# Attention heads and the first feed-forward pair cycle in another order, and a head's output processed in halves

## The chip, the cores and the metric

The kernel runs on one core of one Trainium2 chip. The metric is the device time of one execution in microseconds (us). A core has a matrix engine (TensorE, PE in the profile), three elementwise engines (VectorE = DVE, ScalarE = ACT, GpSimd = POOL) and queues for transfers; SyncE (SP) only issues transfers. The engines run at the same time, and wait for each other by semaphores.

## The reference

Two layers of an encoder over 576 tokens (512 of a prompt and 64 of a sample that also reads 128 cached keys), width 1024, in float32. Each layer is an attention part and a SwiGLU part:

```python
# layer 0: 8 latent-attention heads (mla) and 8 differential heads (diff) side by side
x = x + concat(mla(norm(x)), diff(norm(x))) @ w_out
x = x + (silu(norm(x) @ w_gate) * (norm(x) @ w_up)) @ w_down
# layer 1: 8 heads that attend to the keys an indexer selected (dsa)
x = x + dsa(norm(x)) @ w_out
x = x + (silu(norm(x) @ w_gate) * (norm(x) @ w_up)) @ w_down
# inside a diff head, after its two softmax maps were combined into one (p0 + (-lam) p1):
b_out = rmsnorm(b_out, g_subln, 1e-5) * (1 - lam_init)
```

## The kernel before

The program is written out by hand for each engine: five streams of instructions in program order, joined by semaphores. All of an engine's order is the order in which the code calls its functions. Nothing is reordered.

**Precision.** A float32 matrix product is made of three passes. Every operand is split into a high part (`WH`, `Qh`, `Kh`, `Vh`, `MIXh`, `HH`, made by ACT with a copy) and a low part (`WL`, `Ql`, `Kl`, `Vl`, `MIXl`, subtracted by POOL or DVE), and PE adds high x high, low x high and high x low in an accumulator. 576 tokens are two halves of 288 (`HALF`), so a pass over one weight tile is a pair of matmuls, shown as 128x288 x2.

**Heads.** Heads 0 to 7 are mla, 8 to 15 diff, 16 to 23 dsa. `attention(h)` runs in 8 slots. In slot s it makes the scores of token tile s (`head_scores`, result `S`), turns the probabilities `PR` of an earlier tile by transposes (`T<-IDN,PR`, line 1457 for the last tile), and projects a piece of the next head's q, k or v from its weights (`prepare`, line 1206; tables `CHUNKS`). In other slots come the output projection tiles of an earlier pair of heads (`output_tile`, added to `X` on DVE), the transposes of the next head's keys (`keys_to_tokens`: its new keys `YK` and the cached keys `KC`), and for diff heads the sum and root of the sub-norm (`subnorm_sum`, `subnorm_rows`). A projection leaves PSUM by DVE (`write_projection` to `YQ`, `YK`, `YV`), is split by ACT and POOL (`job`), and only then can scores use it. `acc.group(..., use=...)` picks the PSUM accumulator of a projection (ACC0, ACC1), which must be read out before its next use. DVE also takes row maxima (line 2659), the two maps' combination (`mix_maps`, line 2677) and low parts (`PTl`, line 2684). POOL issues the loads of the cached keys of the next head from its own queue (`load_cached_keys`, line 3242).

**End of an attention part (tail).** The last head's output is copied to `BO`, normed in head 15 (line 2709), split into `MIXh` and `MIXl` over all 576 tokens, and multiplied as the second half of the output projection (`second_half`, line 1527).

**Feed-forward part.** It makes the gate (`G`) and up (`U`) products of 22 blocks of the hidden size. The first two blocks are plain products (`PLAIN`), the others are made in pairs by seven products of half-sized sums (Strassen's form): sums of weights (`mix`, named S1 to S4, in `T` and `S`), split into WH and WL (`seven_high` on ACT, `seven_low` on DVE, line 2860), and sums of tokens (`token_sum` into `XD`, split into `TB`, lines 2892 to 2909). ACT copies a finished product to `TC` (`seven_copy`, line 2161). The first pair's cycle must make all four token sums. POOL multiplies silu(gate) `SG` by `U` into `HF` and splits it into `HH`.

Of the kernel before, what the change touches and what calls it, by code (L numbers as in the profile page):

```python
# [202 lines left out]

def build(nc, a, outs, scratch):
# [54 lines left out]

    VALUES_SHORT = (2, 8, 10, 18, 19, 21, 23)  # L260

    def plan_attention(h):
# [5 lines left out]
        for s in range(SLOTS):  # L268
            finished = []
            c = chunks(g)[s] if g is not None else None  # L270
# [25 lines left out]
            if s == 3 and h % 16 and kind_of(h - 1) == "diff":  # L296
                group("bs", h - 1, use=SHORT)
# [9 lines left out]
            if c:  # L307
                what, k0, k1, total = c
                if k0 == 0 and what not in ("v", "ps") or (k0 == 0 and what == "v" and kind_of(g) != "mla"):
                    if kind_of(g) != "mla":  # L310
                        unit(what, g, end=(what, g), in_slot=True)
                    elif what == "q":
                        unit("q", g, cols=QLT * P, end=("q", g), in_slot=True)
                    elif what == "k":
                        unit("kv", g, cols=2 * KLT * P, end=("v", g), in_slot=True)
                    else:
                        unit("pe", g, cols=2 * QLT * P, end=("ps", g), in_slot=True)
                if k1 == total:
                    group(what, g, use=SHORT if (what == "v" and g in VALUES_SHORT) or (what == "q" and g == 18) else LONG)
                    if kind_of(g) != "mla":  # L320
                        finished.append((what, g))
                    elif what in ("q", "v", "ps"):
                        finished.append(({"v": "kv", "ps": "pe"}.get(what, what), g))
            if h < 16 and g is not None and s == k_job_slot(g) == 5:
                jobs.add("k", g)
            if out_tile(h, s):
# [5 lines left out]
                group("wo", pair_out, m, use=OUT_PAIRS[h][m] if h in OUT_PAIRS else SHORT)  # L332
            begins.append((("slot", h, s), len(units.names) - 1, set(used_up)))
# [22 lines left out]
    def plan_pairs(layer, part):  # L356
# [17 lines left out]
        for c in range(c0, n + 1):  # L374
# [34 lines left out]
            if this:  # L409
# [4 lines left out]
                add(mixes, "S4", c)  # L414
                add(sums, "c11", c)
# [4 lines left out]
            if this:  # L420
                if c + 1 < n:
# [157 lines left out]
    with ctx:  # L579
# [170 lines left out]
        Y_MADE = {"q": 1, "k": 2, "v": 3}  # L750
        setup_c, setup_d = sem("setup_c"), sem("setup_d")
# [314 lines left out]
        def job_of(name):  # L1066
# [17 lines left out]
            if w == "o":  # L1084
                return BO[:, g % 2, :], MIXh[:, g % 2, :], MIXl[:, g % 2, :]

# [103 lines left out]
        def _(pe):  # L1190
# [324 lines left out]
            def second_half(p, m, low):  # L1515
# [4 lines left out]
                if low:  # L1520
# [3 lines left out]
                for left in (wh,) if low else (wh, wl):  # L1524
                    for b in range(2):
# [1928 lines left out]
```

## Time and profile before

| | before |
|---|---|
| time, median of 3 runs | 1730.51 us (1728.37 to 1733.53) |
| the profiled execution: time | 1732.16 us |
| its span in the profile | 1730.3 us |
| PE busy | 1678.6 us, 97% |
| DVE, ACT, POOL busy | 64%, 46%, 34% |
| mean granted PE clock | 0.992 of full speed |

The span is what the profiler saw of the execution; 1.9 us of the time lie outside it. The granted clock is the TensorE clock in parts of full speed. In the timelines a row ends with the idle time ahead of it and the instruction that ended it. A wait for several semaphores is put down to the one that came last by the profile, and that name can be wrong.

### The profile page before, as it was taken

To read this page: it belongs to the slowest core of one execution; us is meant where nothing else is said; L and a number is where in the kernel's file an instruction comes from. 1 tells how busy PE (TensorE), PEld (TensorE's weight loads), DVE (VectorE), ACT (ScalarE), POOL (GpSimd) and SP (SyncE) were. 2 spreads that over 40 slices of the span, in tenths; PEclk is the share of its full clock that TensorE was granted. 3 is DMA by queue.
4 is the path that set the end of the run, shared out by engine and by line. 5 is a ranking of instruction groups with operands and counts; after the bars stand their busy time and mean duration, and the time that the engine had idled before them with its cause. 6 is when DMAs were issued, how large, how long until landed. Compare 5 with 4: busy or idle time off the path is not lost.

```text
span 1730.3 us, 31752 instructions
## 1 busy us (share of the span) xinstructions
PE 1678.6 (97%) x12337; PEld 1617.3 (93%) x12345; DVE 1114.3 (64%) x2086; ACT 803.5 (46%) x1522; POOL 584.6 (34%) x442
## 2 busy tenths in 40 slices
PE   7999999999999999999999999999999999999998
PEld 6889999889898899999999999899989999999998
DVE  4656655555556698478467679633457974884776
ACT  4355555354545555245335445543456551552453
POOL 3344344355443122012102248474451230121122
PEclk9999999999999999999999999999999999999999
DMA  7221132332233123223323242332322332333231
GB/s 195 61 54 56 52 98 68 85 83 73 73 87 91 49 62 110 86 73 98 110 62 100 55 115 69 97 95 78 94 85 67 86 110 62 98 107 89 74 90 64
DMA packets 252104, 145.45 MB, mean 84 GB/s; under 512 B 21934, under 2 KB 242156, under 8 KB 251956
## 3 DMA queue, kind: packets, MB, share of 16 engines
q1 hardware_dynamic: 247080, 135.41, 27.6%
q0 software_dynamic: 4032, 7.77, 1.7%
q8 instruction: 100, 1.64, 0.4%
q14 instruction: 48, 0.39, 0.1%
q10 hardware_dynamic: 844, 0.24, 0.1%
HBM read 130.69 MB, written 15.32 MB: 84 GB/s over the span
## 4 chain that ended last, share of the span: by engine, by line
PE 82%; DVE 10%; ACT 3%; issue 3%; POOL 1%; DMA 1%; SPq 0%; DVEq 0%; ACTq 0%
PE ACC L1206 39%; PE ACC L1586 7%; PE ACC L1588 7%; PE ACC L1587 7%; PE T L1206 3%; PE ACC L1467 2%; PE S L1442 2%; PE S L1206 2%; DVE SCO L2732 2%; DVE TOP L2729 1%; ACT PR L2016 1%; PE S L1588 1%; PE S L1586 1%; PE S L1587 1%; PE S L1418 1%
## 5 line engine op out<-in xcount | busy, mean ns | idle before, releaser
L1206 PE MATMUL ACC<-XGh,WH 128*128 128x288 f32 x1024 | 233.6, 310 | 7.5 <-DVE YK L2585 2.1
L3170 POOL TENSOR_TENSOR WL<-RAW,WH 128x1024 fp32r<-128x1024 f32 (+3 forms) x84 | 180.4, 2150 | 156.9 <-ACT WH L1892 156.7
L3320 POOL TENSOR_TENSOR HF<-SG,U 128x576 f32<-128x576 f32 x44 | 66.6, 1515 | 477.7 <-ACT SG L2189 412.1
L1206 PE MATMUL ACC<-XGh,WL 128*128 128x288 f32 x1024 | 221.0, 298 | 0.0
L1206 PE MATMUL ACC<-XGl,WH 128*128 128x288 f32 x1024 | 220.6, 297 | 0.0
L1586 PE MATMUL ACC<-TB,WH 128*128 128x288 f32 x640 | 189.9, 297 | 5.1 <-DVE WL L2860 4.5
L1892 ACT ACTIVATE WH<-RAW 128x1024 fp32r<-128x1024 f32 (+3 forms) x159 | 153.1, 971 | 81.7 <-PE ACC L1206 43.7
L1588 PE MATMUL ACC<-TB,WL 128*128 128x288 f32 x640 | 189.4, 296 | 0.0
L1587 PE MATMUL ACC<-TB,WH 128*128 128x288 f32 x640 | 189.1, 296 | 0.0
L1206 PE MATMUL ACC<-HH,WH 128*128 128x288 f32 x1032 | 179.3, 295 | 0.0
L1206 PEld LDWEIGHTS ACC<-XGh,WH 128*128 128x128 f32 x1024 | 163.7, 191 | 14.2 <-DVE YK L2585 2.6
L1206 PEld LDWEIGHTS ACC<-XGh,WL 128*128 128x128 f32 x1024 | 165.9, 190 | 0.0
L1206 PEld LDWEIGHTS ACC<-XGl,WH 128*128 128x128 f32 x1024 | 165.8, 190 | 0.0
L1206 PEld LDWEIGHTS ACC<-HH,WH 128*128 128x128 f32 x1032 | 151.3, 188 | 0.0
L2016 ACT ACTIVATE PR<-SX,STAT 128x128 f32<-128x128 f32 (+4 forms) x160 | 85.7, 536 | 131.2 <-DVE STAT L2659 127.6
L1586 PEld LDWEIGHTS ACC<-TB,WH 128*128 128x128 f32 x640 | 120.8, 189 | 6.6 <-DVE WL L2860 4.9
L2423 DVE TENSOR_TENSOR X<-ACC,X 128x576 f32<-128x576 f32 x89 | 66.7, 752 | 89.1 <-PE ACC L1206 85.2
L2407 DVE TENSOR_TENSOR WL<-RAW,WH 128x1024 fp32r<-128x1024 f32 (+2 forms) x75 | 96.3, 1285 | 41.9 <-ACT WH L1892 41.6
L1588 PEld LDWEIGHTS ACC<-TB,WL 128*128 128x128 f32 x640 | 121.1, 189 | 0.0
L1587 PEld LDWEIGHTS ACC<-TB,WH 128*128 128x128 f32 x640 | 121.0, 189 | 0.0
L3322 POOL TENSOR_TENSOR HH<-HF,HH 128x576 fp32r<-128x576 f32 x44 | 67.8, 1541 | 137.6 <-ACT HH L2198 137.6
L1206 PE MATMUL ACC<-HH,WL 128*128 128x288 f32 x516 | 110.1, 294 | 0.0
(459 smaller groups left out, 4342.3 us busy)
## 6 DMA issues: line engine op xcount, KB each, us to landing
RAW<-in_w_gate_dram SPq DMA_DIRECT2D x44, 512.0 KB, 3.9
RAW<-in_w_up_dram SPq DMA_DIRECT2D x44, 512.0 KB, 4.6
RAW<-in_w_down_dram SPq DMA_DIRECT2D x32, 512.0 KB, 4.1
RAW<-in_w_in_even_dram SPq DMA_DIRECT2D x29, 512.0 KB, 5.1
RAW<-in_w_in_odd_dram SPq DMA_DIRECT2D x28, 512.0 KB, 4.4
RAW<-in_w_out_even_dram SPq DMA_DIRECT2D x16, 512.0 KB, 4.2
RAW<-in_w_down_dram SPq DMA_DIRECT2D x16, 384.0 KB, 3.5
RAW<-in_w_out_odd_dram SPq DMA_DIRECT2D x8, 512.0 KB, 5.0
```

Of the source, the lines that this page charges most:

```text
L1206: ins = pe.matmul(out[0:m, 512 * b:512 * b + width], left, right[:, b * width:(b + 1) * width], start=(first and part == 0), stop=(last an ...
L1442: ins = pe.matmul(out[0:r, 0:w], left, right, start=(i == 0), stop=(i == len(products) - 1))
L1586: pe.matmul(out, hi[:, w], xh, start=first and k == 0, stop=False, skip_group_check=not first)
L1587: pe.matmul(out, hi[:, w], xl, start=False, stop=False, skip_group_check=not first)
L1588: ins = pe.matmul(out, lo[:, w], xh, start=False, stop=k == 3, skip_group_check=not first)
L1892: act.activation(WH[slot][:, 0:n], RAW[slot][:, 0:n], ACT.Copy).then_inc(w_hi, 1)
L2016: act.activation(PR[m][0:r, n % 2, 0:w], SX[m][0:r, 0:w], ACT.Exp, bias=STAT[0:r, n % 2, m:m + 1], scale=-1.0, accum_out=STAT[0:r, n % 2, ...
L2407: dve.tensor_tensor(WL[slot][:, 0:n], RAW[slot][:, 0:n], WH[slot][:, 0:n].bitcast(F32), ALU.subtract).then_inc(w_lo, 1)
L2423: return lambda out: dve.tensor_tensor(two(X[:, m, :]), halves(out), two(X[:, m, :]), ALU.add)
L3170: pool.tensor_tensor(WL[slot][:, 0:n], RAW[slot][:, 0:n], WH[slot][:, 0:n].bitcast(F32), ALU.subtract).then_inc(w_lo_pool, 1)
L3320: pool.tensor_tensor(HF[:, q, :], SG[:, q, :], U[:, q, :], ALU.mult).then_inc(h_out, 1)
L3322: pool.tensor_tensor(HH[:, m, 1, :], HF[:, q, :], HH[:, m, 0, :].bitcast(F32), ALU.subtract).then_inc(h_lo, 1)
```

## The change

Nine places change; the arithmetic and the number of matmul passes do not.

1. Head 0: the q projection of head 1 goes ahead of the scores of slot 0 (`share_first`), and the q projection of head 2 moves from head 1's slot 0 to head 0's slot 5 (`share`). Accumulators of k of head 1 and q of heads 2 and 18 are chosen by `SHORT_TOO`.
2. Diff heads: POOL issues the load of the next head's cached keys behind the split of Vl instead of ahead of it.
3. Diff heads 8 to 14 write `YK` in slot 5 ahead of the turned probabilities' low part (`keys_early`).
4. Head 15: the sub-norm sum of head 14 moves behind the output tile of slot 3; its slot 5's addition to X goes ahead of `PTl`.
5. Head 16: the chunk v (4:6) of head 18 goes ahead of the scores of slot 3, and `YK` is written a slot later.
6. Head 22: the addition to X of slot 5 goes ahead of `PTl`.
7. Both tails: the last head's output is normed, split and multiplied in two halves of the tokens.
8. First pair cycle: the copies of the two plain `U` blocks go from DVE to ACT; token sum 3 and the next WG split go ahead of other DVE work; ACT copies the second product to `TC` ahead of S4's split.
9. POOL's first HF waits until the four token sums are split (`tb_lo`).

```diff
+def share(h, s):
+    if (h, s) == (0, 5):
+        return 2, "q", 0, QLT, QLT
+    g = prepared_in(h)
+    if g is None or (h, s) == (1, 0):
+        return None
+    c = chunks(g)[s]
+    return c and (g, *c)
+def share_first(h, s):
+    return (h, s) in ((0, 0), (16, 3))
...
             def attention(h):                              # PE
                 for s in range(SLOTS):
+                    c = share(h, s)
+                    if share_first(h, s):
+                        prepare(*c[:4])
                     if s < TOK_TILES:
                         head_scores(h, s)
...
-                    if g is not None and chunks(g)[s]:
-                        what, k0, k1, _ = chunks(g)[s]
-                        prepare(g, what, k0, k1)
+                    if c and not share_first(h, s):
+                        prepare(*c[:4])
...
+                    if (h, s) == (15, 3):
+                        subnorm_sum(14)
...
                 for low in (False, True):                  # PE, tail
-                    for m in range(halved):
-                        second_half(h - 1, m, low)
+                    for b in range(2):
+                        for m in range(halved):
+                            second_half(h - 1, m, low, b)
...
+            def take_plain_up(layer, m):                   # ACT
+                act.wait_ge(acc_done, acc.made("u", layer, m))
+                act.wait_ge(acc_free, acc.made("g", layer, m))
+                act.activation(two(U[:, m, :]), halves(pair(acc.at("u", layer, m))), ACT.Copy).then_inc(acc_free, 1)
...
-                return s == 5 and (h in (2, 4, 6) or h == 23)
+                return s == 5 and h in (2, 4, 6, 15, 22, 23)
+
+            def keys_early(h, s):                          # DVE
+                return s == 5 and kind_of(h) == "diff" and prepared_in(h) is not None
...
+            def last_norm(h):                              # DVE, tail
+                dve.wait_ge(acc_done, acc.made("bb", h))
+                rows = pair(acc.at("bb", h))
+                for b, (signal) in enumerate((tail_out, acc_free)):
+                    c = slice(b * HALF, (b + 1) * HALF)
+                    dve.scalar_tensor_tensor(out=BO[:, h % 2, c], in0=BO[:, h % 2, c], scalar=GSUB[:, 0:1],
+                                             in1=rows[:, c], op0=ALU.mult, op1=ALU.mult).then_inc(signal, 1)
...
-                    if s == 4 and x is not None and kind_of(h) != "mla" and h != 16:   # POOL
+                    if s == 4 and h > 16 and x is not None:
                         load_cached_keys(x)
...
                     if s == 4 and early_output(h) is not None:
                         job("o", early_output(h))
+                    if s == 4 and x is not None and kind_of(h) == "diff":
+                        load_cached_keys(x)
...
+                        if m == 0 and not part:
+                            pool.wait_ge(tb_lo, 4 * layer + 4)
```

On PE, at the start of head 0 (`QGh` is the latent of q, `WH_55` the weights of head 1's q), the order before is:

```order
L1345 MATMUL T<-IDN_67,BO_85 128x64
L1442 MATMUL S<-Kh_98,Qh0_94 128x128
L1442 MATMUL S<-Kl_99,Qh0_94 128x128
L1442 MATMUL S<-Kh_98,Ql0_96 128x128
L1442 MATMUL S<-KPEh_105,QPE_114 128x128
L1442 MATMUL S<-KPLE_106,QPE_114 128x128
L1344 MATMUL T<-IDN_67,YL_132 128x128 x2
L1345 MATMUL T<-IDN_67,BO_85 128x64
L1344 MATMUL T<-IDN_67,YL_132 64x128 x2
L1345 MATMUL T<-IDN_67,BO_85 64x64
L1206 MATMUL ACC0<-QGh_110,WH0_55 128x288 x2
L1206 MATMUL ACC0<-QGl_111,WH0_55 128x288 x2
```

and of the changed kernel, from the last of the three times that the projection's three passes are issued:

```order
L1235 MATMUL ACC0<-QGh_110,WH0_55 128x288 x2
L1235 MATMUL ACC0<-QGl_111,WH0_55 128x288 x2
L1235 MATMUL ACC0<-QGh_110,WL0_58 128x288 x2
L1471 MATMUL S<-Kh_98,Qh0_94 128x128
L1471 MATMUL S<-Kl_99,Qh0_94 128x128
L1471 MATMUL S<-Kh_98,Ql0_96 128x128
L1471 MATMUL S<-KPEh_105,QPE_114 128x128
L1471 MATMUL S<-KPLE_106,QPE_114 128x128
L1373 MATMUL T<-IDN_67,YL_132 128x128 x2
```

The nine rows of the projection, which began behind the transposes of `YL`, now stand ahead of the five rows of scores. The line numbers of the second fence are those of the changed file, here and below.

On POOL, in head 8, slots 4 and 5, the order before is:

```order
L3177 TENSOR_TENSOR Ql1_97<-YQ_91,Qh1_95 128x576
L3170 TENSOR_TENSOR WL0_58<-RAW0_52,WH0_55 128x1024
L3242 DMA KC_104<-in_cache_diff_k_dram 128x128
L3177 TENSOR_TENSOR Vl_101<-VF_102,Vh_100 128x768
L3170 TENSOR_TENSOR WL1_59<-RAW1_53,WH1_56 128x1024
```

and of the changed kernel:

```order
L3268 TENSOR_TENSOR Ql1_97<-YQ_91,Qh1_95 128x576
L3261 TENSOR_TENSOR WL0_58<-RAW0_52,WH0_55 128x1024
L3268 TENSOR_TENSOR Vl_101<-VF_102,Vh_100 128x768
L3333 DMA KC_104<-in_cache_diff_k_dram 128x128
L3261 TENSOR_TENSOR WL1_59<-RAW1_53,WH1_56 128x1024
```

The load of `KC` and the split of `Vl` change places; behind them stands a `WL` split in both.

On ACT, in the first pair cycle of layer 0, from the split of S12 on, the order before is:

```order
L2181 ACTIVATE WH1_56<-T 128x1024
L2203 ACTIVATE TB_148<-XD_146 128x1152
L2161 ACTIVATE TC_144<-ACC0 128x288
L2181 ACTIVATE WH2_57<-S 128x512
L2181 ACTIVATE WH3_62<-RAW1_53 128x512
L2181 ACTIVATE WH0_55<-RAW2_54 128x1024
L2181 ACTIVATE WH2_57<-S 128x512
L2161 ACTIVATE TC_144<-ACC0 128x288
```

and of the changed kernel:

```order
L2228 ACTIVATE WH1_56<-T 128x1024
L2301 ACTIVATE U_142<-ACC1 128x576
L2250 ACTIVATE TB_148<-XD_146 128x1152
L2208 ACTIVATE TC_144<-ACC0 128x288
L2228 ACTIVATE WH2_57<-S 128x512
L2228 ACTIVATE WH3_62<-RAW1_53 128x512
L2228 ACTIVATE WH0_55<-RAW2_54 128x1024
L2208 ACTIVATE TC_144<-ACC0 128x288
L2250 ACTIVATE TB_148<-XD_146 128x1152
L2228 ACTIVATE WH2_57<-S 128x512
```

A copy of `U` is new, and the second `TC` copy, which stood behind the split of S4 (the second `WH2_57<-S`), now stands ahead of it and of the last `TB`.

## Rows read from the trace of the kernel before

**Rows 1.** The page: the span's line, and the engines' busy time.
```profile
span 1730.3 us, 31752 instructions
...
PE 1678.6 (97%) x12337; PEld 1617.3 (93%) x12345; DVE 1114.3 (64%) x2086; ACT 803.5 (46%) x1522; POOL 584.6 (34%) x442
```

**Rows 2.** Windows: stretch, busy time per engine (instructions), granted clock, DMA share, GB/s.
```profile
87.70:94.50 6.80, 6.80 (x30) 5.86 (x29) 3.18 (x7) 1.31 (x4) 1.63 (x2) 0.50 0.37 68
...
558.70:562.10 3.40, 3.40 (x19) 2.90 (x19) 2.82 (x12) 1.49 (x5) 0.00 (x0) 0.50 0.71 170
...
1357.40:1360.80 3.40, 3.40 (x15) 3.40 (x16) 3.31 (x3) 1.58 (x2) 0.00 (x0) 0.51 1.00 287
```

**Rows 3.** The same view, line 1206 alone, two stretches of 3.8 us.
```profile
89.70:93.50 3.80, 3.80 (x16) 3.80 (x17) 0.50 0.46 83
77.00:80.80 3.80, 3.80 (x31) 3.80 (x31) 1.00 0.36 109
```

**Rows 4.** Timeline of PE, heads 0 and 1: start, duration, operation, idle before, releaser.
```profile
87.20 0.30 PE L1442 MATMUL S<-Kh,Qh 128*128 128x128 f32 x1 [1.45 <-POOL Ql L3177]
...
105.15 0.21 PE L1457 MATMUL T<-IDN,PR 64*64 64x64 f32 x1 [1.73 <-ACT PR L2024]
...
105.70 0.33 PE L1442 MATMUL S<-Kh,Qh 128*128 128x128 f32 x1 [0.28 <-POOL Kl L3177]
```

**Rows 5.** Timeline of DVE, POOL and PE in head 8.
```profile
303.62 4.75 DVE L2677 SCALAR_TENSOR_TENSOR PR<-PR,STAT,PR 64x192 f32<-64x192 f32 x1
...
304.00 1.85 POOL L3177 TENSOR_TENSOR Vl<-VF,Vh 128x768 fp32r<-128x768 f32 x1
305.80 2.35 POOL L3170 TENSOR_TENSOR WL<-RAW,WH 128x1024 fp32r<-128x1024 f32 x1
...
308.52 0.21 PE L1457 MATMUL T<-IDN,PR 64*64 64x64 f32 x1 [2.08 <-DVE PR L2677]
...
309.69 0.85 PE L1206 MATMUL ACC<-XGh,WH 128*128 128x288 f32 x2 [0.89 <-DVE YK L2585]
```

**Rows 6.** Timeline of DVE and PE in head 10, slots 4 and 5.
```profile
378.55 1.11 DVE L2677 SCALAR_TENSOR_TENSOR PR<-PR,STAT,PR 64x192 f32<-64x192 f32 x1
...
382.67 0.53 PE L1206 MATMUL ACC<-XGh,WH 128*128 128x288 f32 x2 [0.39 <-DVE YK L2585]
```

**Rows 7.** Head 9: POOL, PE, and the page's line on KC's transfers.
```profile
350.62 1.85 POOL L3177 TENSOR_TENSOR Vl<-VF,Vh 128x768 fp32r<-128x768 f32 x1 [2.91 <-ACT Vh L1923]
...
353.97 0.27 PE L1372 MATMUL T<-IDN,KC 128*128 128x128 f32 x1
...
KC<-in_cache_diff_k_dram POOLq DMA_DIRECT2D x8, 64.0 KB, 3.4
```

**Rows 8.** Timeline of PE and DVE, head 15 and layer 0's tail.
```profile
556.46 1.23 PE L1214 MATMUL ACC<-ONES,SQ 128*128 128x1 f32 x10 [0.67 <-ACT SQ L2042]
...
568.68 1.52 PE L1222 MATMUL ACC<-IDN,RS 128*128 128x128 f32 x10 [1.21 <-DVE X L2423]
...
580.08 0.81 DVE L2709 SCALAR_TENSOR_TENSOR BO<-BO,GSUB,ACC 128x576 f32<-128x576 f32 x1 [1.92 <-PE ACC L1222]
...
581.75 0.50 PE L1527 MATMUL T<-MIXh,WH 128*128 128x288 f32 x2 [1.71 <-ACT MIXh L1923]
```

**Rows 9.** Timeline of DVE, ACT and PE, each layer's first pair cycle.
```profile
625.95 2.58 DVE L2909 TENSOR_TENSOR TB<-XD,TB 128x1152 fp32r<-128x1152 f32 x1
...
630.39 0.41 ACT L2161 ACTIVATE TC<-ACC 128x288 f32<-128x288 f32 x1
...
630.90 0.37 PE L1586 MATMUL ACC<-TB,WH 128*128 128x288 f32 x1 [2.25 <-DVE WL L2860]
...
633.28 0.40 PE L1586 MATMUL ACC<-XGh,WH 128*128 128x288 f32 x1 [0.56 <-DVE WL L2860]
...
1357.26 0.42 PE L1586 MATMUL ACC<-TB,WH 128*128 128x288 f32 x1 [2.26 <-DVE WL L2860]
```

**Rows 10.** Timeline of PE, head 16, slot 3.
```profile
1096.62 0.46 PE L1442 MATMUL S<-Kh,Qh 128*128 128x512 f32 x1 [2.33 <-DVE SEL L2739]
```

More of the change, by code:

```diff
@@ L414, in plan_pairs @@
                 add(mixes, "S4", c)
+                if not before and not part:
+                    add(seven_lo, "WG", c + 1)
                 add(sums, "c11", c)
@@ L420, in plan_pairs @@
             if this:
-                if c + 1 < n:
+                if c + 1 < n and (before or part):
                     add(seven_lo, "WG", c + 1)
@@ L1524, in second_half @@
                 for left in (wh,) if low else (wh, wl):
-                    for b in range(2):
-                        right = (MIXl if low else MIXh)[:, 1, b * HALF:(b + 1) * HALF]
-                        ins = pe.matmul(out[:, 512 * b:512 * b + HALF], left[:, cols], right, start=False, stop=low)
-                if low:
+                    right = (MIXl if low else MIXh)[:, 1, b * HALF:(b + 1) * HALF]
+                    ins = pe.matmul(out[:, 512 * b:512 * b + HALF], left[:, cols], right, start=False, stop=low)
+                if low and b:
                     ins.then_inc(acc_done, 1)
@@ L2218, in cycle @@
                     ahead(layer, part, 1, "P5")
-                if c >= 2 and (before or part):
+                if c >= 2 and (part or c > PLAIN + 1):
                     hidden_hi(layer, part, c - 2)
+                if not part and c == PLAIN + 1:
+                    hidden_hi(layer, part, 0)
                 if this:
@@ L2234, in cycle @@
                         ahead(layer, part, 0, "P2")
+                    if not before and not part:
+                        seven_copy("t2", layer, part, c)
+                        token_sum_hi(layer, 3, 1)
                     seven_high("S4", layer, part, c)
-                    seven_copy("t2", layer, part, c)
-                    if not before and not part:
-                        token_sum_hi(layer, 3, 1)
+                    if before or part:
+                        seven_copy("t2", layer, part, c)
                 else:
@@ L2925, in cycle @@
                         seven_low("S3", layer, part, c)
+                    if not before and not part:
+                        token_sum(layer, 3)
                     mix("S4", layer, part, c)
+                    if not before and not part:
+                        seven_low("WG", layer, part, c + 1)
                     add_up("c11", layer, part, c)
                     seven_low("A22", layer, part, c)
-                    if not before and not part:
-                        token_sum(layer, 3)
                 if before:
@@ L2934, in cycle @@
                 if this:
-                    if c + 1 < n:
+                    if c + 1 == n:
+                        begin("ahead", layer, part, 0)
+                    elif before or part:
                         seven_low("WG", layer, part, c + 1)
-                    else:
-                        begin("ahead", layer, part, 0)
                     if not before and not part:
@@ L2984, in ffn @@
                 begin("u", layer, 0)
-                evacuate(("u", layer, 0), lambda out: dve.tensor_copy(two(U[:, 0, :]), halves(out)))
                 token_sum(layer, 1)
@@ L2988, in ffn @@
                 token_sum_lo(layer, 1, 1)
+                dve.wait_ge(acc_free, acc.made("u", layer, 0))
                 evacuate(("g", layer, 1), times(G[:, 1, :], RSTD))
@@ L2993, in ffn @@
                 seven_low("S12", layer, 0, PLAIN)
-                evacuate(("u", layer, 1), lambda out: dve.tensor_copy(two(U[:, 1, :]), halves(out)))
                 mix("S3", layer, 0, PLAIN)
@@ L3015, in ffn @@
                             dve.wait_ge(sg_done, hidden.made(layer, part, n - 1))
+                            dve.wait_ge(acc_free, acc.made("u", layer, 1))
                         if m >= 2:
```

101 lines of the change are left out of this document (69 added, 32 removed).

## The prediction, made before the changed kernel ran

> **What bounds the kernel now.** I read the page first. PE is busy for 1678.6 of 1730.3 us [rows 1], so 51.7 us of idle time are all that any order can win, beside time in which PE is busy but slow. Then I read the granted clock in windows, because a mean of 0.992 hides short stretches. The trace has one stretch of 6.8 us in head 0 at 0.50 and then five of 3.4 us, at 309.6, 558.7, 582.6, 1098.0 and 1357.4; three rows stand for the six [rows 2]. 0.50 is the level of 1.2 GHz, where the rest is at 2.4 GHz. What this costs is seen in line 1206 alone: 16 matmuls start in 3.8 us at 0.50, and 31 in 3.8 us at 1.00 [rows 3]. So a stretch costs half its length: 3.4 us in head 0, 1.7 us at each of the others. Each begins some 0.1 to 2.3 us behind the end of an idle time of PE (0.5 us in head 0, 2.2 us in head 15, 0.1 us at 1357.4); but the 1.73 us at 105.15 [rows 4] and the 2.25 us at 630.90 [rows 9] are followed by none. Filling an idle time may therefore win a stretch too, and need not.
>
> Last I read PE's timeline for idle times with their releasers, and at each one the other engines' rows. The change touches eight of the largest.
>
> **The change, part by part.**
>
> *Heads 0 and 1.* Scores wait 1.45 us for Ql, and behind them comes the slow stretch, in which the nine pairs of head 1's q run [rows 4, 2]. At 8 pairs in 3.8 us they take 4.3 us; at 15.5 pairs in 3.8 us they take 2.2 us [rows 3]. Put ahead of the scores they fill the 1.45 us and push the scores back by 0.75 us, and the 4.3 us behind are gone: 3.5 us won. DVE must still copy the transposes out and rotate q before the next scores, and now has less cover: I take 3.0 (bounds 0.7, if the slow stretch comes all the same, and 4.85, the idle time and half of 6.8). Head 2's q, again 2.2 us, now stands where PE waits 1.73 and then 0.28 us [rows 4]: 2.0 (bounds 0 and 2.01). Together 5.0.
>
> *Head 8.* The combination of the two maps takes 4.75 us on DVE, from 303.62 to 308.37, for 64x192 elements, where it took 1.11 us in head 10 [rows 5, 6]. It reads two SBUF tiles. POOL runs Vl from 304.00 and WL from 305.80 to 308.15 [rows 5], and the DVE row ends just behind the second. So DVE was held for both, and 0.15 us behind its end PE goes on. The order now is Vl, KC's load, WL. Vl then starts some 0.5 us earlier, ends near 305.3, and the load's issue parts it from WL, so that the combination can run near 305.7 us, ahead of PE's need: PE had work until 308.52 - 2.08 = 306.44. The wait of 0.89 us for YK [rows 5] goes because YK is written ahead of PTl. With the slow stretch at 309.6 that is 2.08 + 0.89 + 1.7 = 4.7; I take 4.0, since DVE has PTl, YK and an addition to do in the same 2 us (bounds 0.9 and 4.7).
>
> The Trainium skill, "SBUF — State Buffer", section "Who interferes with whom", says that a VectorE instruction with two SBUF inputs contends with a GpSimd instruction that reads SBUF, and that who issues first holds the shared ports for the whole instruction. The row of 4.75 us agrees, and shows DVE losing twice in a row. By this rule alone the sum would be the same here, but it speaks against the change in heads 10, 12 and 14 (below).
>
> *Heads 10, 12 and 14.* PE waits 0.39 us for YK in each, one row for three [rows 6]. YK now stands ahead of PTl: 3 x 0.39 = 1.2 (bounds below nothing, see the rival, and 1.2).
>
> *Head 9.* The load of KC now goes out behind Vl, which ends at 350.62 + 1.85 = 352.47. From issue to landing the median is 3.4 us, so KC is there at 355.9; PE turns it at 353.97 [rows 7]: a new wait of 1.9 us. I take 1.7 as loss (bounds 0, if it lands in 1.5 us, and 3.6, with a slow stretch behind it). In the other heads Vl ends by more than the 3.4 us ahead of PE's turn of KC.
>
> *Head 15 and the tail.* The 0.67 us ahead of the sum of squares go, as two output pairs now stand ahead of it; the 1.21 us at 568.68, where PE waits for an addition to X, go because that addition stands ahead of PTl [rows 8]. With the slow stretch at 558.7 [rows 2] that is 3.6; I take 2.9, since the single-column matmuls and their transposes stay (bounds 1.0 and 3.6). In the tail PE waits from 580.04 to 581.75 for a norm of 0.81 us and a split over all tokens [rows 8]. Halved, the norm's first half is about 0.4 us sooner and the split's 0.3: 0.6 after the extra instructions; the slow stretch behind I leave (bounds 0 and 2.3). Tail 23 has no such wait; I count nothing.
>
> *First pair cycle.* PE waits 2.25 and 0.56 us in layer 0, 2.26 us in layer 1 [rows 9]. The releaser is given as DVE's WL, but the wait is for several, and ACT's copy to TC of the product in ACC0, the accumulator that PE writes next, ends at 630.39 + 0.41 = 630.80, 0.10 us ahead of PE. That copy stands behind the split of S4, and S4 behind DVE's late chain, in which the split of TB took 2.58 us [rows 9] while POOL worked on HF. The new order takes the copy out from behind S4, moves HF behind the last TB, and gives two copies of U to ACT. DVE then has two copies of U and at least the 1.2 us of the held TB less ahead of this point in each layer, and all three waits lack their cause. With the slow stretch at 1357.4 the bound is 2.25 + 0.56 + 2.26 + 1.7 = 6.8. HF and HH are not gone but run later, where DVE again has two-input work; the row of 2.58 us, twice its like, prices such a meeting at 1.2 us. Two such meetings in a layer, a third of which reaches PE, cost 0.8: I take that off in each and count 5.2 (bounds 0 and 6.8).
>
> *Heads 16, 22.* The 2.33 us for the selection [rows 10] are filled with a chunk of 1.6 us, but the selection's chain through exponents goes on from the same moment, and PE soon waits for it: 0.6 (bounds 0 and 2.3). Head 22: nothing counted, 0.5 possible.
>
> Sum: 5.0 + 4.0 + 1.2 - 1.7 + 2.9 + 0.6 + 5.2 + 0.6 = 17.8 us. From the profiled execution's 1732.16 us this gives 1714.4; it lay 1.65 us above the median of the runs, so the median forecast is 1712.7 us.
>
> **The rivals.** *A, the clock does not follow.* Some 7 us of the sum are slow stretches (about 2.6 in head 0, 1.4 in head 8, 1.2 in head 15, 1.7 in layer 1). Idle times of 1.73 and 2.25 us brought none, so where one comes is partly chance, and new short waits may bring others. Then 1712.7 + 7 = 1720.
>
> *B, the first pair cycles still wait.* If HF and HH, or ACT with its two more copies, hold the next products, 5.2 us fall away: 1718. For it speaks that both DVE and ACT are in one chain there; against it, that nothing reads HF soon.
>
> *C, on the other side: POOL's held port.* In heads 9 to 14 Vl now follows WL without the issue of a load between. In head 10 the combination ran at 378.55 for 1.11 us [rows 6], that is, it got in only where WL had ended. If it must wait for Vl too, a head loses what head 8 lost: 2.08 + 0.89 + 1.7 = 4.7 us with its stretch, or 1.4 us where PE has other work. In the three even heads this is 4 to 14 us: 1717 to 1727. It decides from four heads on (4 x 4.7 = 18.8, the whole gain); slower than before by a measurable amount takes five. The rule quoted above is what would do it; that POOL's boundary let DVE in where it was already waiting speaks against five such heads.
>
> **How the numbers follow.** The forecast 0.60 (its own range 1706 to 1718), A 0.17, B 0.13, C 0.10, of which 0.04 are five heads or more. No change means within 0.3% (5.2 us), about what a measurement of this kernel can tell. Slower is 0.04 from C; the same is 0.06 (0.03 from C, 0.03 where A and B fall together); faster 0.90. The low end takes all upper bounds but about 5 us: 1706. The high end takes in A with B, 1725.
>
> **What the profile after would show.** No slow stretch in head 0 and PE at work up to its first scores; in head 8 a combination of under 2 us; a wait ahead of KC's transposes in head 9 of 1 to 2 us; no wait over 0.5 us in both first pair cycles, with HF behind the fourth TB; one slow stretch in the tail of layer 0. The prediction is wrong if combinations of over 2 us appear in heads 10, 12 and 14, if slow stretches stand elsewhere in the same number, or if PE's idle time falls by less than 8 us.

## The result, and the profile after

| | before | changed |
|---|---|---|
| time, median | 1729.68 us (4 runs, 1728.37 to 1733.53) | 1714.53 us (4 runs, 1713.4 to 1715.3) |
| ratio, 95% interval | | 0.9907 (0.9892 to 0.9923) |
| profiled execution: time | 1732.16 us | 1713.77 us |

The changed kernel is faster by 0.93%. The forecast was 1712.7 us. The page of the changed kernel, first the span's line, then the engines' busy time:

```profile
span 1712.0 us, 31779 instructions
...
PE 1670.0 (98%) x12337; PEld 1609.6 (94%) x12345; DVE 1108.3 (65%) x2084; ACT 805.9 (47%) x1528; POOL 581.6 (34%) x444
```

Against [rows 1] the span is 18.3 us shorter, PE's busy time 8.6 us and its idle time 9.7 us. So nearly half of the gain is not idle time, but work that took less time. Most of that is the granted clock. The windows of the changed kernel show it (columns as in [rows 2]; the clock stands third from the end):

```profile
83.00:92.00 9.00, 9.00 (x63) 8.23 (x62) 6.01 (x17) 4.19 (x10) 4.43 (x3) 1.00 0.27 45
297.00:300.40 3.40, 3.40 (x27) 3.17 (x26) 3.01 (x6) 1.85 (x4) 3.40 (x2) 1.00 0.32 99
547.30:554.10 6.80, 5.36 (x23) 5.35 (x24) 2.98 (x8) 4.92 (x10) 4.16 (x2) 0.50 0.01 2
569.30:572.70 3.40, 3.35 (x25) 3.38 (x26) 0.95 (x2) 1.45 (x3) 1.56 (x2) 1.00 0.00 0
1090.00:1093.40 3.40, 3.40 (x16) 3.40 (x15) 0.46 (x3) 1.84 (x4) 2.92 (x4) 0.50 0.24 69
1346.50:1349.90 3.40, 3.37 (x25) 3.38 (x26) 3.26 (x5) 3.40 (x8) 2.68 (x2) 1.00 0.00 0
```

The stretches of head 0, head 8, the tail of layer 0 and layer 1's first pair cycle are at 1.00 now. Two slow stretches are left ahead of the program's last microseconds: the old one of head 16 and a new one of 6.8 us in head 15. Before there were six with 23.8 us, now two with 10.2 us. PE was busy for 23.7 us of the six and for 8.8 us of the two (in head 15 it stood idle for part of the stretch), so at half speed some 7.5 of the 8.6 us are the clock.

The time from one head's last transposes of PR to the next head's, taken in both traces, is out of line with the prediction in four places: heads 7, 9 and 15 and the tail of layer 0. These are rows of heads 0, 8, 10 and 9 (PE, DVE, DVE, PE): the start, the duration, the operation, and at the end of a row the idle time ahead of it and its releaser.

```profile
96.76 0.63 PE L1484 MATMUL T<-IDN,PR 128*128 128x128 f32 x4 [0.87 <-ACT PR L2060]
...
294.70 1.88 DVE L2737 SCALAR_TENSOR_TENSOR PR<-PR,STAT,PR 64x192 f32<-64x192 f32 x1
...
365.89 1.11 DVE L2737 SCALAR_TENSOR_TENSOR PR<-PR,STAT,PR 64x192 f32<-64x192 f32 x1
...
341.29 0.30 PE L1401 MATMUL T<-IDN,KC 128*128 128x128 f32 x1 [0.60 <-DMA KC<-in_cache_diff_k_dram]
```

In head 0, 0.87 us are left of the waits of 1.73 and 0.28 us [rows 4]. DVE's combination in head 8 takes 1.88 us instead of 4.75 [rows 5], in head 10 it takes 1.11 us as before [rows 6], and KC comes late in head 9, by 0.60 us.

From head 6's last transposes of PR to head 7's it is 0.9 us less, beside an edit that the list of nine places leaves out. DVE's split of the next weights, which stood in slot 5 of head 6, now comes in slot 6, behind an addition to X. In the kernel before it stood ahead of that addition, and PE waited (DVE, PE):

```profile
245.19 1.52 DVE L2407 TENSOR_TENSOR WL<-RAW,WH 128x1024 fp32r<-128x1024 f32 x1
...
247.69 0.53 PE L1206 MATMUL ACC<-XGh,WH 128*128 128x288 f32 x2 [0.67 <-DVE X L2423]
```

The changed kernel has no such wait there. No run tried this edit by itself, so that it is the cause is read from these rows alone.

Head 15 and the tail, PE but for the third row, which is DVE's:

```profile
543.74 1.15 PE L1243 MATMUL ACC<-ONES,SQ 128*128 128x1 f32 x10
...
548.74 0.85 PE L1235 MATMUL ACC<-MIXh,WH 128*128 128x288 f32 x2 [2.95 <-DVE RS L2496]
...
548.54 0.14 DVE L2496 TENSOR_SCALAR RS<-ACC 64x1 f32<-64x1 f32 x1
...
569.35 0.37 PE L1558 MATMUL T<-MIXh,WH 128*128 128x288 f32 x1 [1.17 <-ACT MIXh L2180]
```

Here is what went wrong. The sub-norm sum of head 14 is issued at 543.74 and no longer waits. But the next output tile waits 2.95 us until DVE has read that sum from its accumulator (548.54), and a slow stretch of 6.8 us begins within this wait, at 547.3 us. In the tail PE waits 1.17 us where it waited 1.71 [rows 8].

The first pair cycles, DVE for three rows, PE for three, POOL for one:

```profile
602.13 1.22 DVE L2949 TENSOR_TENSOR WL<-RAW,WH 128x1024 fp32r<-128x1024 f32 x1
603.45 1.36 DVE L2998 TENSOR_TENSOR TB<-XD,TB 128x1152 fp32r<-128x1152 f32 x1
...
610.50 1.36 DVE L2998 TENSOR_TENSOR TB<-XD,TB 128x1152 fp32r<-128x1152 f32 x1 [0.62 <-ACT TB L2250]
...
621.64 0.40 PE L1621 MATMUL ACC<-XGh,WH 128*128 128x288 f32 x1 [0.23 <-DVE U L2969]
...
1346.53 0.40 PE L1621 MATMUL ACC<-XGh,WH 128*128 128x288 f32 x1 [0.22 <-DVE U L2969]
...
602.06 0.40 PE L1235 MATMUL ACC<-XGh,WH 128*128 128x288 f32 x1 [0.27 <-ACT U L2301]
...
617.83 1.43 POOL L3420 TENSOR_TENSOR HF<-SG,U 128x576 f32<-128x576 f32 x1 [46.97 <-DVE TB L2998]
```

A WL and two TB rows take 1.22, 1.36 and 1.36 us, where one TB took 2.58 us [rows 9]; PE's waits of 2.25, 0.56 and 2.26 us have become 0.23 and 0.22 us, and POOL's first HF starts behind the fourth TB. A small wait is new: 0.27 us at 602.06 for ACT's copy of a plain `U` block, ahead of layer 0's first pair cycle. Last, head 16 on PE:

```profile
1080.52 0.46 PE L1471 MATMUL S<-Kh,Qh 128*128 128x512 f32 x1 [0.73 <-DVE SEL L2799]
...
1085.32 0.63 PE L1484 MATMUL T<-IDN,PR 128*128 128x128 f32 x4 [0.90 <-ACT PR L2060]
1087.05 0.21 PE L1486 MATMUL T<-IDN,PR 64*64 64x64 f32 x1 [1.10 <-ACT PR L2060]
...
1088.18 0.33 PE L1401 MATMUL T<-IDN,KC 128*128 128x128 f32 x1 [0.85 <-DVE PTl L2744]
```

The wait for the selection fell from 2.33 us [rows 10] to 0.73 us, and waits of 0.90, 1.10 and 0.85 us stand behind it, where the kernel before had one of 1.13 us (at 1105.40, for `PTl`).

### The profile page after: what moved, and what is told of

Same layout as the page of the kernel before. It is cut to its first block, busy times and chain, and to the rows that moved or that the text cites. A ratio compares the mean times of both kernels' runs of the same rounds, so it can differ in the third digit from the quotient of the medians.

```text
span 1712.0 us, 31779 instructions
## 1 busy us (share of the span) xinstructions
PE 1670.0 (98%) x12337; PEld 1609.6 (94%) x12345; DVE 1108.3 (65%) x2084; ACT 805.9 (47%) x1528; POOL 581.6 (34%) x444
## 4 chain that ended last, share of the span: by engine, by line
PE 81%; DVE 11%; ACT 4%; issue 3%; POOL 1%; DMA 0%; ACTq 0%; DVEq 0%
PE ACC L1235 40%; PE ACC L1621 7%; PE ACC L1623 7%; PE ACC L1622 7%; PE T L1235 3%; PE ACC L1496 2%; PE S L1235 2%; PE S L1471 2%; DVE SCO L2792 2%; ACT PR L2052 1%; DVE TOP L2789 1%; PE S L1623 1%; PE S L1621 1%; PE S L1622 1%; PE T L1484 1%
```

## Experiments

A time with a ratio is a median of four executions, with its ratio to the kernel before on the same chip and the 95% interval. A time without a ratio (experiments 5 to 11) is one execution, and there only the rows count. "Turn to turn" is the time from the last transposes of PR of one head to those of the next.

**1. The sum in the other accumulator** (`h15_other_acc`).

```diff
             if (h, s) == (15, 3):
-                group("bs", 14, use=SHORT)
+                group("bs", 14, use=LONG)
```

> The changed kernel with one word changed: the sub-norm sum of head 14, behind the output tile of slot 3, gets the other accumulator (use=LONG). Theory (the sum took the accumulator that the next output tile needs, and DVE reads the sum late): PE's idle time of 2.95 us in head 15 and the slow stretch behind it go, head 15 is 3 to 4.7 us shorter, the time 1711 us. Rival (PE waits there for DVE's work whatever the accumulator): the wait stays over 2 us and the time at 1714.5.

1712.73 us, 0.9895 (0.9880 to 0.9910). PE's row in head 15:

```profile
546.70 1.26 PE L1243 MATMUL ACC<-ONES,SQ 128*128 128x1 f32 x10 [2.14 <-DVE X L2483]
```

The wait did not go, it moved: the output tile of slot 3 has just used that accumulator, and the sum itself now waits 2.14 us for DVE's addition to X. Head 15, turn to turn, takes 34.7 instead of 36.2 us: 1.5 us less, where 3 to 4.7 were expected, and the wait of over 2 us is the one that the rival named. So the theory holds only in that the accumulator decides who waits. With the sum behind the tile, both accumulators are in DVE's hands.

**2. The sum in its old place** (`h15_old_order`). PE's `subnorm_sum(14)`, the plan's group and DVE's `b_mean(14)` stand in slot 3 again, ahead of the output tile.

```diff
-                    if s == 3 and h in (9, 11, 13):
+                    if s == 3 and h in (9, 11, 13, 15):
                         subnorm_sum(h - 1)
...
-                    if (h, s) == (15, 3):
-                        subnorm_sum(14)
```

> The changed kernel with the sub-norm sum of head 14, and DVE's reading of it, back in their old places (ahead of the output tile of slot 3). Theory: a wait of 0.67 us for the square returns, the 2.95 us go: 1711.5 to 1713, with or without a slow stretch of 1.7. If the wait of 2.95 us comes from the addition to X that was moved in slot 5, it stays.

1712.34 us, 0.9891 (0.9874 to 0.9907).

```profile
543.95 1.23 PE L1241 MATMUL ACC<-ONES,SQ 128*128 128x1 f32 x10 [0.67 <-ACT SQ L2074]
```

The 0.67 us are back as expected, the 2.95 us gone, and head 15 takes 32.5 us, 3.8 us less than in the changed kernel. A slow stretch of 3.4 us follows; this window lies in it:

```profile
547.00:549.00 2.00, 2.00 (x13) 1.50 (x13) 1.86 (x6) 0.43 (x2) 0.00 (x0) 0.50 0.70 171
```

The time falls by only 2.2 us, since from head 15's turn to head 17's it takes 1.3 us more than in the changed kernel: the slow stretch of head 16 is 6.8 us long in this trace. The addition to X in slot 5 is early here too, so it was not the cause.

**3. DVE reads the sum sooner** (`h15_read_early`). The sum stays behind the tile; only the reading moves from slot 4 to the end of slot 3. Head 9's load is as in experiment 4.

```diff
-                    if s == (3 if h in (9, 11, 13) else 4) and h % 16 and kind_of(h - 1) == "diff":
+                    if s == (3 if h in (9, 11, 13) else 4) and h % 16 and h != 15 and kind_of(h - 1) == "diff":
                         b_mean(h - 1)
...
+                    if (h, s) == (15, 3):
+                        b_mean(14)
```

> The changed kernel with head 9's load as before, head 15's sub-norm sum left in its new place, and DVE's reading of that sum moved up from slot 4 to the end of slot 3. Theory (the 2.95 us are PE waiting for a late reading of the accumulator, nothing else): the wait falls under 1 us, head 15 takes 31 to 32.5 us, the time 1710 to 1712. Rival (DVE is late at this place anyway, and reads no sooner): a wait of 2 us or more stays, here or at the next use of DVE's work, and head 15 takes 34 us or more.

1710.20 us, 0.9880 (0.9864 to 0.9896).

```profile
546.64 0.53 PE L1235 MATMUL ACC<-MIXh,WH 128*128 128x288 f32 x2 [0.39 <-DVE RS L2496]
```

The wait is 0.39 us, the releaser the same reading of `RS`, now early. There is no slow stretch, and head 15 takes 31.2 us. This settles the cause: in its new place the sum needed its reader moved along with it. It also shows that the new place wins nothing: with the sum in its old place and head 9's load as here, head 15 takes 31.3 us (experiment 4).

**4. Head 9's load back ahead of Vl, on top of experiment 2** (`h15_h9_old`).

```diff
-                    if s == 4 and h > 16 and x is not None:
+                    if s == 4 and (h > 16 or h == 9) and x is not None:
                         load_cached_keys(x)
...
-                    if s == 4 and x is not None and kind_of(h) == "diff":
+                    if s == 4 and x is not None and kind_of(h) == "diff" and h != 9:
                         load_cached_keys(x)
```

> The changed kernel with head 15's sub-norm sum in its old place, as before, and in head 9 alone the load of the cached keys ahead of Vl, as before. Theory (the load behind Vl lands late in head 9 only): the wait of 0.60 us for KC goes and head 9 is 0.8 us shorter, with the other heads unchanged: 1711.5 us. Rival (the load's place does nothing, head 9's 0.8 us come from elsewhere): head 9 stays as in the changed kernel.

1710.12 us, 0.9880 (0.9860 to 0.9900), beside experiment 3 the fastest. Head 10, which begins with head 9's late keys, takes 29.7 us from turn to turn instead of 30.5: the 0.8 us are back. The clock in head 15 came as a surprise (windows of the same kernel):

```profile
541.00:545.00 4.00, 3.34 (x27) 2.73 (x24) 3.22 (x9) 2.99 (x8) 0.00 (x0) 1.00 1.12 322
545.00:549.00 4.00, 4.00 (x35) 3.71 (x34) 3.46 (x14) 2.42 (x8) 0.00 (x0) 1.00 0.57 138
549.00:553.00 4.00, 3.55 (x26) 3.07 (x25) 1.86 (x4) 3.97 (x8) 2.94 (x2) 1.00 0.00 0
```

Head 15's code is that of experiment 2, where the clock fell to 0.50 at 546.3 us. Here it is 1.00 throughout, with a wait of 0.66 us ahead of the sum. Head 15 takes 31.3 instead of 32.5 us. The sum is reached 1.4 us earlier (542.58 and 543.95 us); whether that is what decides was not tried.

**5. Head 8's load alone, on the kernel before** (`h8_load_behind`).

```diff
-                    if s == 4 and x is not None and kind_of(h) != "mla" and h != 16:
+                    if s == 4 and x is not None and kind_of(h) != "mla" and h not in (8, 16):
                         load_cached_keys(x)
                     if s == v_job_slot(h):
                         job("v", h)
...
+                    if h == 8 and s == 4:
+                        load_cached_keys(x)
```

> The kernel before with one edit: in head 8 alone POOL issues the load of the cached keys behind Vl. Theory (POOL's Vl and WL back to back hold DVE's combination): it falls from 4.75 to some 2 us, PE's wait of 2.08 us goes; the wait for YK (0.89 us) is reached earlier and is 0.5 to 1.5 us. Head 8 is 1.5 to 3.5 us shorter. Rival (the port does not matter, DVE is held by something else): the row stays over 4 us.

1725.04 us. DVE's combination:

```profile
300.61 1.87 DVE L2677 SCALAR_TENSOR_TENSOR PR<-PR,STAT,PR 64x192 f32<-64x192 f32 x1
```

It takes 1.87 us, and the slow stretch at 309.6 us [rows 2] has no counterpart in this trace. From head 7's turn to head 9's the kernel needs 71.7 us, where the kernel before needs 76.0 and the changed one 71.5. So 4.3 of the 4.5 us at this place come from one issue on POOL, more than the 1.5 to 3.5 us expected. The wait for YK went with it, without `keys_early`: the expectation of 0.5 to 1.5 us left there was wrong.

Heads 0 and 1 of this kernel are those of the kernel before. There, with the same wait of 1.45 us ahead of the scores, the slow stretch is 3.4 us long and not 6.8:

```profile
87.40:90.80 3.40, 3.40 (x15) 3.40 (x16) 1.70 (x4) 0.81 (x2) 1.51 (x1) 0.51 0.42 77
90.80:94.20 3.40, 3.40 (x27) 3.40 (x26) 2.17 (x7) 1.09 (x4) 0.00 (x0) 0.99 0.42 97
```

**6. Head 0's scores first again** (`scores_first`).

```diff
-    return (h, s) in ((0, 0), (16, 3))
+    return (h, s) == (16, 3)
```

> The changed kernel with the scores of head 0's slot 0 ahead of head 1's q projection again. Theory (the idle time ahead of the scores brings the slow stretch): a wait of 1.4 us ahead of the scores, granted clock 0.50 for 3.4 to 6.8 us behind it; the end of head 0 comes 2.5 to 4 us later than in the changed kernel. Rival (the gain of 5.9 us there is the moved q projection of head 2 alone): under 1 us later.

1717.32 us. PE's row of the scores, and two windows with the clock behind it:

```profile
85.60 0.30 PE L1471 MATMUL S<-Kh,Qh 128*128 128x128 f32 x1 [1.45 <-POOL Ql L3268]
...
86.20:89.60 3.40, 3.40 (x17) 2.70 (x17) 2.00 (x6) 1.31 (x4) 1.69 (x2) 0.60 0.26 51
89.60:93.00 3.40, 3.40 (x26) 3.40 (x26) 1.60 (x4) 0.47 (x2) 0.35 (x1) 0.90 0.47 92
```

The start-up ahead of head 0 varies by 2 us and more between executions, so I count from the first single-column sums of the latents' norm (PE, `S<-ONES,SQL`: 71.92 us before, 69.51 changed, 70.33 here) to head 0's turn: 33.2 us before, 32.4 here, 30.2 in the changed kernel. The projection ahead of the scores is worth 2.2 us, a little under the expected span; a slow stretch comes back, of 3.4 us and not 6.8. To head 1's turn, counted in the same way, it is 53.76 us before, 50.33 here, 48.15 in the changed kernel, and 52.29 in experiment 5, where heads 0 and 1 are as before and the slow stretch is 3.4 us too. So of the 5.6 us of heads 0 and 1, 2.2 are this projection and 2.0 head 2's (52.29 less 50.33). The other 1.5 us are the second half of the stretch of 6.8 us, which the same code has in one trace and not in the other.

**7. The copy to TC alone, on the kernel before** (`tc_copy_first`).

```diff
+                    if not before and not part:
+                        seven_copy("t2", layer, part, c)
                     seven_high("S4", layer, part, c)
-                    seven_copy("t2", layer, part, c)
+                    if before or part:
+                        seven_copy("t2", layer, part, c)
```

> The kernel before with one edit: in the first pair cycle of each layer ACT copies the second product to TC ahead of the split of S4. Theory (PE waits for this copy, not for DVE's WL that the profile names): the wait of 2.25 us falls to 0.5 to 0.8 us (the next to come is WL of S3), that of 0.56 us grows to some 2 us, since DVE's WG split is as late as before; together 0 to 0.5 us less. Rival (PE waits for DVE's WL at 630.14): 2.25 and 0.56 stay as they are.

1731.93 us.

```profile
628.10 0.40 PE L1586 MATMUL ACC<-TB,WH 128*128 128x288 f32 x1 [0.54 <-DVE WL L2863]
...
632.19 0.40 PE L1586 MATMUL ACC<-XGh,WH 128*128 128x288 f32 x1 [2.24 <-DVE WL L2863]
...
1356.06 0.40 PE L1586 MATMUL ACC<-TB,WH 128*128 128x288 f32 x1 [0.56 <-DVE WL L2863]
...
1360.15 0.40 PE L1586 MATMUL ACC<-XGh,WH 128*128 128x288 f32 x1 [2.23 <-DVE WL L2863]
```

In both layers the first wait falls to 0.54 and 0.56 us and the second is 2.24 and 2.23 us. (In layer 1 the kernel before showed no second wait: PE was in its slow stretch there, and came later.) So PE did wait for ACT's copy, which PE's row does not name; and taking this wait away by itself is worth nothing, since DVE's WL for the next product is as late as before.

**8. HF at once** (`hf_at_once`).

```diff
                         pool.wait_ge(sg_done, made)
-                        if m == 0 and not part:
-                            pool.wait_ge(tb_lo, 4 * layer + 4)
```

and ACT splits HF where it did before.

> The changed kernel in which POOL does not wait for the fourth token sum before it makes HF, and ACT splits HF as early as before. Theory (POOL's HF and HH hold DVE's two-input work of the chain): a WL of 2.46 us and a TB of 2.6 us come back, each 1.2 us over its like, and PE waits 1 to 2.5 us again in each layer's first pair cycle: 2 to 5 us slower than the changed kernel. Rival (the two U copies and the order on DVE and ACT were enough): the two long rows come back, but PE's waits stay under 0.5 us.

1716.65 us. DVE and PE in layer 0's first pair cycle:

```profile
604.45 2.40 DVE L2995 TENSOR_TENSOR TB<-XD,TB 128x1152 fp32r<-128x1152 f32 x1
...
611.96 2.59 DVE L2995 TENSOR_TENSOR TB<-XD,TB 128x1152 fp32r<-128x1152 f32 x1
...
618.20 0.40 PE L1621 MATMUL ACC<-XGh,WH 128*128 128x288 f32 x1 [0.54 <-DVE WL L2946]
...
620.53 0.37 PE L1621 MATMUL ACC<-TB,WH 128*128 128x288 f32 x1 [0.48 <-DVE TB L2995]
```

TB takes 2.40 and 2.59 us again, and PE waits 0.54 and 0.48 us; in layer 1 it is 0.69 and 0.48. The WL that was expected to grow to 2.46 us keeps its 1.22. The delay of HF is worth 0.8 us in layer 0 and 0.95 in layer 1, together a little under the 2 to 5 us expected.

**9. The U copies on DVE** (`u_on_dve`).

```diff
-                take_plain_up(layer, 0)
...
+                evacuate(("u", layer, 0), lambda out: dve.tensor_copy(two(U[:, 0, :]), halves(out)))
```

and the same for the second block.

> The changed kernel with the two copies of the plain U blocks on DVE again, everything else kept. Theory (the copies on ACT are half of what freed DVE's chain, and HF's delay the other): waits of 0.5 to 1.5 us a layer come back in the first pair cycle, 1 to 3 us in all. Rival (the order of the copy to TC and the delay of HF are enough): no wait over 0.3 us, the same time as the changed kernel.

1714.68 us.

```profile
618.44 0.37 PE L1621 MATMUL ACC<-TB,WH 128*128 128x288 f32 x1 [0.48 <-DVE TB L2996]
...
622.23 0.40 PE L1621 MATMUL ACC<-XGh,WH 128*128 128x288 f32 x1 [0.38 <-DVE U L2967]
```

The waits are 0.48 and 0.38 us, against one of 0.23: 0.6 us a layer, the same in layer 1. As expected, and small. The wait of 0.27 us for ACT's copy, new in the changed kernel, is gone here. Still PE comes to the second of these rows 0.6 us later than in the changed kernel (621.64 us), with head 15's turn at the same time in both.

**10. Head 16 as before** (`h16_old`).

```diff
-    return (h, s) in ((0, 0), (16, 3))
+    return (h, s) == (0, 0)
```

and YK written in slot 3.

> The changed kernel with head 16's chunk behind the scores of slot 3 and YK written in slot 3, as before. Theory (the selection's chain sets the pace there, so that the filled 1.6 us come back as waits of 0.90, 1.10 and 0.85 us): the wait for the selection is 2.3 us, the three others are under 1.2 us together, and heads 16 and 17 take as long as in the changed kernel within 0.7 us. Rival (the edit gains): 1 us or more longer.

1714.31 us.

```profile
1081.27 0.47 PE L1471 MATMUL S<-Kh,Qh 128*128 128x512 f32 x1 [2.31 <-DVE SEL L2799]
...
1087.81 0.21 PE L1486 MATMUL T<-IDN,PR 64*64 64x64 f32 x1 [0.60 <-ACT PR L2060]
...
1088.92 0.33 PE L1401 MATMUL T<-IDN,KC 128*128 128x128 f32 x1 [0.83 <-DVE PTl L2744]
```

The wait for the selection is 2.31 us again, and the waits behind it 0.60 and 0.83 us, together 1.4 where under 1.2 us were expected. From head 15's turn to head 17's it takes 556.10 us in both kernels: this part of the change is worth nothing.

**11. PE waits for both halves in the tails** (`tail_wait_both`).

```diff
-                if b == 0:
-                    pe.wait_ge(tail_lo if low else tail_hi, tails(p + 1))
-                elif low:
+                if low:
```

> The changed kernel in which PE waits in the tails for both halves of MIXh, and of MIXl, before the second half of the output projection; the norms and splits stay in halves. Theory (the first half's earlier start is what the halves win): PE starts 0.4 us later in layer 0's tail (a wait of 1.6 instead of 1.17 us), under 1 us in all, and more only if a slow stretch follows the longer wait (1.7). Rival (the halves win nothing, the split is not what PE waits for): the wait stays 1.17 us.

1715.12 us.

```profile
570.42 0.37 PE L1556 MATMUL T<-MIXh,WH 128*128 128x288 f32 x1 [1.60 <-ACT MIXh L2180]
```

The wait is 1.60 us against 1.17. Behind it the clock is at 0.50, as in the kernel before and not in the changed one:

```profile
572.00:574.00 2.00, 2.00 (x10) 2.00 (x9) 0.43 (x1) 0.00 (x0) 0.00 (x0) 0.50 0.00 0
```

So from head 15's turn to head 16's it takes 1.5 us more.

## Why the prediction was right, and where not

The time, 1714.53 us, is 1.8 us above the forecast and inside its own range; the gain against the median before that the forecast used is 16.0 us of 17.8 (against the median of all four runs it is 15.2). That it came so near is in part luck: single terms are off by up to 4.7 us, and their errors cancel to 0.6 us. The terms, with the measured ones from the two traces:

| place | forecast | measured |
|---|---|---|
| heads 0 and 1 | 5.0 | 5.6 |
| head 8 | 4.0 | 4.5 |
| heads 10, 12, 14 | 1.2 | 1.0 |
| head 9's load | -1.7 | -0.8 |
| head 15 up to the tail | 2.9 | -1.8 |
| tail of layer 0 | 0.6 | 2.2 |
| first pair cycles | 5.2 | 6.1 |
| heads 16 and 17 | 0.6 | about -0.5 |
| head 7, not forecast | 0 | 0.9 |

- **Heads 0 and 1** came as forecast in the sum. Experiments 5 and 6 give 2.2 for the first part (3.0 forecast) and 2.0 for the second, as forecast; 1.5 us are the length of one slow stretch, which differs between traces of the same code.
- **Head 8**: experiment 5 shows that POOL's order is the cause, and alone worth 4.3 us. That it acts through a held port is read from the rows (the combination ends just behind POOL's instructions); no run separates it from other ways in which POOL could hold DVE.
- **Heads 10, 12, 14 and rival C**: the combination takes 1.11 or 1.12 us as before. That is not its time alone, since it takes 0.40 or 0.41 us in heads 9, 11 and 13; but nothing was added. In head 15 it takes 1.17 us instead of 0.40. PE's wait of 0.39 us is gone, as forecast.
- **Head 9**: the wait came at the forecast place with 0.60 us, since the load landed 2.17 us after its issue (338.98 to 341.15 us) and not the median of 3.4 us: the size was off, inside its bounds. Experiment 4 gives it back.
- **Head 15 is the step that failed.** The prediction said that "the 0.67 us ahead of the sum of squares go", and counted the slow stretch with them: 2.9 us won up to the tail, where 1.8 were lost. It looked at what PE waits for ahead of the moved sum, and not at who needs the sum's accumulator next. Turn to turn head 15 became 3.3 us longer; 1.5 us came back where the addition to X is now early. Experiments 1 to 3 show the cause: PE writes the next tile into the accumulator that DVE reads only in slot 4. Even with the reader moved too, the new place of the sum wins nothing against the old one (31.2 and 31.3 us, experiments 3 and 4), so this term was at best the slow stretch and the addition to X.
- **Tail**: the halves gave 0.54 us, as the 0.6 forecast. The other 1.7 us are the slow stretch, which the forecast had left standing. Experiment 11 fits this: with 0.43 us more of waiting the stretch is there again. So do the other traces: each of the four with a wait of 1.60 or 1.71 us at this place has the stretch, and none of the nine with 1.17 or 1.18 us. For tail 23 nothing was counted. From head 22 to layer 1's first pair cycle some 0.8 us are lost, and PE has a new wait in the tail, for an addition to X:

```profile
1296.92 0.40 PE L1235 MATMUL ACC<-MIXh,WH 128*128 128x288 f32 x1 [0.45 <-DVE X L2483]
```

- **First pair cycles**: PE waited for ACT's copy and not for the WL that the profile names (experiment 7). All of the bound of 6.8 came but 0.7 us, of which 0.45 are small waits. Of the causes, HF's delay measures some 0.9 us a layer and the U copies some 0.6; the rest, some 1.1 us of waits in layer 0, and 0.5 us of waits and the slow stretch in layer 1, is left to the order of token sum 3, WG and the copy, which was not tried by itself with DVE relieved.
- **Heads 16 and 17**: experiment 10 makes the edit of head 16 worth nothing. The selection's chain sets the pace, as the prediction said, but entirely. The 0.5 us lost against the kernel before are lost in experiment 10 too, so they have another cause, which stays open.
- **Head 7** was not forecast; the edit that its rows point to is named with them.
- **Rival A** did not come as a whole: 13.6 us of slow stretches went, worth some 7 us, against some 7 counted. But they went elsewhere than forecast, in head 0 and the tail for more, in head 15 for less than nothing.
- **The signs**: as said beforehand, head 0 has no slow stretch, the combination of head 8 is under 2 us, no wait in the first pair cycles is over 0.5 us, and HF comes behind the fourth TB. Two were wrong: the wait for KC in head 9 is 0.60 us and not 1 to 2, and the tail of layer 0 has no slow stretch. None of the three that would have made the prediction wrong came: PE's idle time fell by 9.7 us.

The terms add up to 17.2; with some 2.4 us by which the latents' norm ahead of head 0 came sooner in the second trace (71.92 and 69.51 us), and some 1.3 us lost in small pieces, this is the 18.3 us between the spans. The small pieces are some 0.6 us ahead of the first pair cycle of layer 0, where the new wait of 0.27 us stands, and the 0.8 us around tail 23. The start varies between executions of the same kernel, so I don't put it down to the change.

Putting head 9's load and head 15's sum right gives 1710.1 to 1710.2 us (experiments 3 and 4), 4.3 to 4.4 us under the changed kernel and 1.2% under the kernel before.

## What to carry to other kernels

When a product is moved in front of or behind another one that shares its accumulator, look up who reads it and when, and move the reader too: the wait that disappears ahead of the product otherwise comes back ahead of the accumulator's next user. Ask also whether the move wins anything once that is done; here it did not. A wait for several semaphores is best priced by asking for each of them when it would have been met; the releaser in the row may be the wrong one, and the next one in line decides what removing the first is worth. Where one engine's long instructions seem to hold another engine, look for two of them back to back, and try another instruction between them. It was worth 4.3 us in head 8; in heads 10, 12 and 14 there was nothing to win.

## What the runs showed of the hardware

The granted clock falls to half for 3.4 us (or 6.8 us) behind or within waits of PE of quite different sizes: none behind 1.73 us at 105.15 [rows 4] or 2.25 us at 630.90 [rows 9] in the trace before, one behind 0.67 us in experiment 2, and none behind 0.66 us at the same place in experiment 4, 1.4 us earlier in the execution. Even the two first are not safe: in experiment 7 a stretch follows the wait of head 0's end (at 103.5 us), and in experiment 5 one follows the wait of 2.26 us in layer 0's first pair cycle (at 623.3 us). In the changed kernel's tail 1.17 us brought none and 1.60 us (experiment 11) one. In these thirteen traces some places are steady all the same: the wait of 1.45 us ahead of head 0's scores has a stretch in four traces of four, the 2.95 us of head 15 in six of six. So a single trace does not price a wait: in head 15 the same code costs 1.2 us more or less from one trace to the other, in heads 0 and 1 it is 1.5 us. And a stretch costs less than half its length where PE has to wait anyway: in the changed kernel's head 15 PE is busy for 5.36 of the 6.8 us.

DVE's combination of two SBUF tiles was held twice in a row: its row begins at 303.62 us, POOL ran 304.00 to 305.85 and 305.80 to 308.15, and it ended at 308.37 [rows 5]. Ahead of the two stands the issue of the load:

```profile
303.42 0.56 POOL L3242 DMA_DIRECT2D KC<-in_cache_diff_k_dram  x1
```

With that issue between the two POOL instructions the combination got in after the first (1.88 us in the changed kernel). The Trainium skill, "SBUF — State Buffer", section "Who interferes with whom", says that a VectorE instruction with two SBUF inputs contends with a GpSimd instruction that reads SBUF, and of the modes that use both ports that who issues first has the shared pair for the whole instruction. The rows agree in that the combination ends only behind POOL's instructions. They do not show that POOL's came first: in head 8 before, the row of the combination begins 0.38 us ahead of Vl's, and whether the load's issue at 303.42 held it until then was not tried. What they also leave open is who is next when GpSimd's instructions follow each other without a break: in head 8 before, the waiting combination lost at 305.80 us; in head 10 of the changed kernel, where POOL's WL ends at 366.79 and Vl starts at 366.75 us, it got in between (365.89 to 367.00 us) and cost PE nothing. Why once and not the other time was not tried. This too shifts between traces: in head 15 the combination takes 0.40 us in the kernel before, but 2.00 us in experiment 5, where the code of head 15 is the same, and PE waits 0.91 us for it.
